# Four modulation row tiles formed by GpSimd in the first feed-forward part instead of by TensorE in the recurrent loop

## The reference, cut to what matters

```python
mod = (silu(c) @ ada_w + ada_b)        # 9 rows of 1024
(sh1, sc1, g1, sh2, sc2, g2, sh3, sc3, g3) = split(mod, 9)
y = rmsnorm(h, ffn1_pre_g) * (1 + sc1) + sh1
h = h + 0.5 * g1 * rmsnorm(swiglu(y), ffn1_post_g)
y = rmsnorm(h, mix_pre_g) * (1 + sc2) + sh2
h = h + g2 * rmsnorm(token_mix(y), mix_post_g)      # 4 mLSTM heads, 4 HGRN heads
y = rmsnorm(h, ffn2_pre_g) * (1 + sc3) + sh3
h = h + 0.5 * g3 * rmsnorm(swiglu(y), ffn2_post_g)
```

## Time and profile before

| what | us |
|---|---|
| timed runs (3): median | 1752.55 |
| timed runs: lowest, highest | 1751.01, 1753.04 |
| profiled execution: span | 1748.8 |
| PE busy in it | 1701.6 (97%) |
| DVE busy | 1133.4 (65%) |
| ACT busy | 791.6 (45%) |
| POOL busy | 349.1 (20%) |

### The profile page before, as it was taken

The page is one execution under the profiler, slowest core; times in us unless marked ns, Lnnn a source line. Parts: engine busy times, 40 slices in busy tenths (PEclk is TensorE's granted clock), DMA queues, the critical chain, the costliest instruction groups (busy, mean ns, idle before and its releaser), DMA issues.

```text
span 1748.8 us, 32936 instructions
## 1 busy us (share of the span) xinstructions
PE 1701.6 (97%) x12844; PEld 1512.7 (87%) x12844; DVE 1133.4 (65%) x1857; ACT 791.6 (45%) x1241; POOL 349.1 (20%) x325
## 2 busy tenths in 40 slices
PE   6999999999999999999899999999999999999997
PEld 3999879977999889877869999999999988888886
DVE  4877557676665455983664699488899644444444
ACT  4334454655454454642234534555544433333334
POOL 2000010111000010000010577600000155555553
PEclk9999999999999999999999999999999999999999
DMA  9877655456565533441044456545555566666664
GB/s 357 294 268 289 217 196 190 144 194 230 192 209 174 193 122 132 158 144 38 3 179 141 131 170 179 168 156 159 161 161 162 169 192 193 192 192 194 194 192 162
DMA packets 64385, 314.42 MB, mean 180 GB/s; under 512 B 7152, under 2 KB 7568, under 8 KB 44688
## 3 DMA queue, kind: packets, MB, share of 16 engines
q1 hardware_dynamic: 62928, 305.94, 52.4%
q10 hardware_dynamic: 1280, 6.82, 1.1%
q0 software_dynamic: 64, 0.04, 0.0%
HBM read 311.72 MB, written 1.05 MB: 179 GB/s over the span
## 4 chain that ended last, share of the span: by engine, by line
PE 89%; DVE 5%; ACT 2%; DMA 2%; issue 1%; POOL 1%; SPq 0%; DVEq 0%; POOLq 0%; ACTq 0%
PE bank L421 25%; PE bank L422 24%; PE bank L423 24%; PE bank L2836 2%; DMA ring<-in_stream 1%; PE bank L2809 1%; DVE ring_rounded L381 1%; PE bank L1378 1%; PE bank L2394 1%; DMA ring<-in_experts 1%; PE bank L782 1%; POOL ring_rounded L3142 1%; PE bank L2407 1%; PE bank L2045 1%; PE bank L596 0%
## 5 line engine op out<-in xcount | busy, mean ns | idle before, releaser
L423 PE MATMUL bank<-yb_rounded,ring_rounded 128*128 128x256 f32 x2000 | 566.0, 283 | 0.0
L2927 ACT CAST ring_rounded<-ring 128x1024 fp32r<-128x1024 f32 x248 | 260.5, 1051 | 281.8 <-DMA ring<-in_experts 281.6
L423 PEld LDWEIGHTS bank<-yb_rounded,ring_rounded 128*128 128x128 f32 x2000 | 383.8, 192 | 0.0
L381 DVE TENSOR_TENSOR ring_rounded<-ring,arena_rounded 128x1024 fp32r<-128x1024 f32 x230 | 270.8, 1220 | 131.3 <-ACT arena_rounded L367 130.8
L421 PE MATMUL bank<-yb_rounded,arena_rounded 128*128 128x256 f32 x1104 | 316.3, 286 | 0.9 <-issue 0.9
L422 PE MATMUL bank<-yT_rounded,arena_rounded 128*128 128x256 f32 x1104 | 313.4, 284 | 0.0
L3102 DVE TENSOR_TENSOR ring_rounded<-ring,ring_rounded 128x1024 fp32r<-128x1024 f32 x128 | 156.9, 1226 | 191.2 <-ACT ring_rounded L2927 191.2
L421 PE MATMUL bank<-yb_rounded,ring_rounded 128*128 128x256 f32 x960 | 278.1, 290 | 2.1 <-POOL ring_rounded L3142 1.2
L367 ACT CAST arena_rounded<-ring 128x1024 fp32r<-128x1024 f32 x230 | 229.0, 1048 | 106.2 <-PE bank L421 98.5
L422 PE MATMUL bank<-yT_rounded,ring_rounded 128*128 128x256 f32 x960 | 271.1, 282 | 0.0
L422 PE MATMUL bank<-ring_rounded,arena_rounded 128*128 128x512 f32 x688 | 267.7, 389 | 0.0
(11 more groups left out here) (439 smaller groups left out, 2646.4 us busy)
## 6 DMA issues: line engine op xcount, KB each, us to landing
ring<-in_stream SPq DMA_DIRECT2D x144, 1024.0 KB, 4.9
ring<-in_experts SPq DMA_DIRECT2D x256, 512.0 KB, 3.5
field<-in_stream SPq DMA_DIRECT2D x24, 512.0 KB, 7.1
field<-in_stream SPq DMA_DIRECT2D x4, 1024.0 KB, 7.0
field<-in_gains ACTq DMA_DIRECT2D x3, 512.0 KB, 7.5
field<-in_gains ACTq DMA_DIRECT2D x1, 1536.0 KB, 6.7
const<-in_const SPq DMA_DIRECT2D x1, 1473.0 KB, 11.5
xh<-in_x ACTq DMA_DIRECT2D x1, 1024.0 KB, 5.5
```

Of the source, the lines that this page charges most:

```text
L381: ins = nc.vector.tensor_tensor(ring_r[:, g % SLOTS, half], ring[:, g % SLOTS, half], top.bitcast(F32), ALU.subtract)
L423: return first, pe.matmul(bank, s_rest, m_top, start=False, stop=stop)
L2927: nc.scalar.copy(expert_top[:, n % E_SLOTS, :], expert_w[:, n % E_SLOTS, :]).then_inc(expert_top_ready, 1)
```

## The change

Tiles 12 to 15 leave the loop. A list `POOLED` takes the place of `LOOPED`. SP fetches their eight chunks, as two halves each, behind the ring chunks of the feed-forward tiles 6, 10, 14, 18, 22, 25, 27 and 29, into two places that are free at that time. GpSimd scales the four pieces of a chunk (TENSOR_SCALAR) and adds them to the row (TENSOR_TENSOR). TensorE's ones-matmuls and ACT's copies for tiles 12, 13 and 14 stand behind tiles 13, 20 and 29; those of tile 15 stand in the mixer, between the last evacuated modulation tile and the mixer's own first chunk. The ring stream is eight chunks shorter between the projections and the output projection.

```diff
-        LOOPED = {0: 12, 2: 13, 4: 14, 5: 15}
+        POOLED = [12, 13, 14, 15]
-        SUM_BEHIND = {6: 4, 10: 5, 14: 6, 18: 7, FT - 1: 8, FT + 4: 9}
+        SUM_BEHIND = {6: 4, 10: 5, 13: 12, 14: 6, 18: 7, 20: 13, FT - 1: 8, FT + 4: 9, FT + 7: 14}
+        POOL_BEHIND = [6, 10, 14, 18, 22, 25, 27, 29]
+        pool_places = [halves((arena4, 1024), (arena2, 0)), halves((arena1, 0), (arena1, HALF))]
+        def row_part_pool(pool, h):
+            tile, c = POOLED[h // 2], h % 2
+            if h == 0:
+                pool.wait_ge(sem("silu_c"), 1)
+                pool.wait_ge(sem("ada_b_in1"), 16)
+            pool.wait_ge(pool_landed[h % 2], 32 * (h // 2 + 1))
+            parts = [pool_places[h % 2][k // 2][:, k % 2 * 512:(k % 2 + 1) * 512] for k in range(4)]
+            for k, w in enumerate(parts):
+                nc.gpsimd.tensor_scalar(w, w, col("c")[:, 4 * c + k:4 * c + k + 1], 1.0, ALU.mult, ALU.mult
+                                        ).then_inc(sem("pool_row_scaled"), 1)
+            for k, w in enumerate(parts):
+                pool.wait_ge(sem("pool_row_scaled"), 4 * h + k + 1)
+                pool.wait_ge(sem("pool_row_step"), 4 * h + k)
+                nc.gpsimd.tensor_tensor(row(tile), row(tile), w, ALU.add).then_inc(sem("pool_row_step"), 1)
         def row_sum_pe(pe, tile):
-            pe.wait_ge(sem("row_step"), 8 * (HOSTED.index(tile) + 1))
+            if tile in POOLED:
+                pe.wait_ge(sem("pool_row_step"), 8 * (POOLED.index(tile) + 1))
+            else:
+                pe.wait_ge(sem("row_step"), 8 * (HOSTED.index(tile) + 1))
...
                 act.wait_ge(sem("rows_scaled"), 1)
+                act.wait_ge(sem("pool_row_step"), 4 * 7)
...
             ada_groups_pe(pe, BEHIND["ffn1"][1])
+            row_sum_pe(pe, POOLED[-1])
...
                 if i:
                     read_out(i - 1)
-                if i in LOOPED:
-                    ada_groups_pe(pe, LOOPED[i])
-                if i - 1 in LOOPED:
-                    ada_sum_pe(pe, LOOPED[i - 1], but=3)
...
             late_groups_act(act, "ffn1")
+            row_sum_act(act, POOLED[-1])
+            mark("pooled_rows", A.free, 4 + A.emptied.n)
...
-            await_mark(dve, "looped_rows")
+            await_mark(dve, "pooled_rows")
...
+                if g in pool_behind:
+                    h = pool_behind.index(g)
+                    if h >= 2:
+                        sp.wait_ge(sem("pool_row_step"), 4 * (h - 1))
+                    for place, half in zip(pool_places[h % 2], (slice(0, HALF), slice(HALF, CHUNK))):
+                        sp.dma_start(place, stream[tile_at(POOLED)[h]][:, half]).then_inc(pool_landed[h % 2], 16)
...
+            for h in range(2 * len(POOLED)):
+                row_part_pool(pool, h)
             own_rest_pool(pool, "mix")
```

More of the change, by code:

```diff
@@ L746, in partial @@
                 return arena3[:, tile * 512:(tile + 1) * 512]
-            where, at = {10: (arena3, 2048), 12: (arena2, 0), 14: (arena2, 1024), 16: (arena2, 0)}[tile - tile % 2]
+            where, at = {10: (arena3, 2048), 16: (arena2, 0)}[tile - tile % 2]
             return where[:, at + tile % 2 * 512:at + tile % 2 * 512 + 512]
@@ L957, in row_part_dve @@
                                                ALU.mult, ALU.add).then_inc(sem("row_step"), 1)
+        POOL_BEHIND = [6, 10, 14, 18, 22, 25, 27, 29]
+        pool_places = [halves((arena4, 1024), (arena2, 0)), halves((arena1, 0), (arena1, HALF))]
+        pool_landed = [sem(f"pool_row_landed{j}") for j in range(2)]
+        def row_part_pool(pool, h):
[12 more added lines that the diff above has]
+                nc.gpsimd.tensor_tensor(row(tile), row(tile), w, ALU.add).then_inc(sem("pool_row_step"), 1)
         def row_sum_pe(pe, tile):
-            pe.wait_ge(sem("row_step"), 8 * (HOSTED.index(tile) + 1))
+            if tile in POOLED:
+                pe.wait_ge(sem("pool_row_step"), 8 * (POOLED.index(tile) + 1))
+            else:
+                pe.wait_ge(sem("row_step"), 8 * (HOSTED.index(tile) + 1))
             bank = A.take(pe)
@@ L1118, in ffn_act @@
                         row_sum_act(act, SUM_BEHIND[i - 2])
-                        mark("hosted_rows", A.free, 4 + A.emptied.n)
+                        if SUM_BEHIND[i - 2] == HOSTED[-1]:
+                            mark("hosted_rows", A.free, 4 + A.emptied.n)
                 act.wait_ge(sem("rows_scaled"), 1)
+                act.wait_ge(sem("pool_row_step"), 4 * 7)
                 top_chunk_act(act, 2)
@@ L1537, in mix_act @@
                     top_chunk_act(act, 8)
-                if i in LOOPED:
-                    ada_groups_act(act, LOOPED[i])
-                if i - 1 in LOOPED:
-                    ada_sum_act(act, LOOPED[i - 1])
-                    mark("looped_rows", A.free, 4 + A.emptied.n)
             a(head_square(last - 1))
@@ L2927, in top_expert @@
                 nc.scalar.copy(expert_top[:, n % E_SLOTS, :], expert_w[:, n % E_SLOTS, :]).then_inc(expert_top_ready, 1)
-            act.wait_ge(begun, stream.shape[0] - len(own_at) - 2 * len(HOSTED))
+            act.wait_ge(begun, stream.shape[0] - len(own_at) - 2 * len(HOSTED + POOLED))
             for _ in range(2):
@@ L3181, in program @@
         source += [rest_at + i for i in (*range(1, 12), 14, 15, 12, 13)]
-        source += tile_at(LOOPED.values()) + list(range(rest_at + 16, rest_at + 20)) + tile_at(BEHIND["mix"])
+        source += list(range(rest_at + 16, rest_at + 20)) + tile_at(BEHIND["mix"])
         source += range(rest_at + 21, mix2_rows)
@@ L3185, in program @@
         source += [*range(mix2_rows + 11, mix2_rows + 29), *range(mix2_rows + 30, stream.shape[0])]
-        assert sorted(source + list(own_rows.values()) + tile_at(HOSTED)) == list(range(stream.shape[0]))
+        assert sorted(source + list(own_rows.values()) + tile_at(HOSTED) + tile_at(POOLED)) == list(range(stream.shape[0]))
         assert len(source) % SLOTS == 0
         row_behind = [split_at[0] + i + 1 for i in ROW_BEHIND]
+        pool_behind = [split_at[0] + i + 1 for i in POOL_BEHIND]
         own_behind = {split_at[FT + 4]: "mix", source.index(rest_at + 16) + 3: "ffn2", source.index(rest_at + 21) + 16: "mix2",
```

## The result

| | before | after |
|---|---|---|
| timed runs (4 each): median, us | 1751.83 | 1772.62 |
| lowest, highest | 1751.01, 1753.04 | 1769.84, 1775.28 |
| span of the profiled execution | 1748.8 | 1771.6 |
| PE busy | 1701.6 | 1703.4 |
| mean granted clock | 0.996 | 0.989 |

What follows compares the result with a forecast made beforehand. It took PE as the bound (89% of the chain), narrowly over DVE in gate/up. GpSimd rows +17, sums +3.0 and loop -7.5 gave +12.5; with 1748.8 and 3.75 carried over, 1765.0 us, range 1752 to 1774.

Steps and rivals of the forecast that it cites:

- rival A: Feed-forward part: DVE is not held up, GpSimd fits into its pauses; -4.5 us, 1748.0 us; 12 in 100.
- The loop, -7.5: Recurrent loop: 14.2 us of PE work go, 5.0 us of DVE idleness stay, so it closes 7.5 us earlier.
- rival B: The loop gives more (-12.5) and GpSimd costs less (+10), sums +3: 1753 us; 10 in 100.
- The sums, +3.0: PE's ones-matmuls: three in the feed-forward part cost 2.6 us, the fourth, in the mixer, 0.4.
- The GpSimd rows, +17: Feed-forward part: GpSimd's eight half tiles hold up DVE and thereby PE, +17 us, bounds 0 and +26.
- 14.4 was forecast: Gate/up part: the halves behind tiles 6, 10, 14 and 18 each cost PE 3.6 us.
- 2.6 was forecast for four halves: Last gate/up tile and down part: the fifth half, behind tile 22, costs 2.6 us, the last three nothing.
- The last three meet a DVE that only splits weights ... and cost nothing: Down part: beside the last three halves DVE is busy only 2.36 us in some 5.5, so cost 0.
- C: Rival: the loop gives nothing, as DVE and the ACT chain take over at once; 1772.5 us; 6 in 100.
- D: Rival: GpSimd's TENSOR_SCALAR is as dear as its TENSOR_TENSOR, rows +26; 1774 us and more; 6 in 100.
- side estimate of 7.1 us held per half tile: Feed-forward part: by the skill's 769 ns per 512 elements, a half tile holds SBUF 7.1 us, against 6.6 taken.
- The DMA queue, 0: Feed-forward part: 8.4 MB more to fetch, +46 GB/s, counted at 0, at most +2 us.

Runs made afterwards that it cites:

- e1: Changed kernel with GpSimd's 64 instructions cut to one column each, fetches, waits and sums kept: 1746.37 us, ratio 0.9978.
- e2: Changed kernel with the 64 GpSimd instructions replaced by as many MEMSETs of 128x1024, which read nothing: 1746.75 us, ratio 0.998.
- e3: Kernel before with its looped tiles and their sums left out altogether: 1742.72 us, ratio 0.9961.
- e5: Changed kernel with GpSimd's 32 additions cut to one column and the 32 scalings whole: 1746.88 us, ratio 0.9982.
- e6: Changed kernel with GpSimd's 32 scalings cut to one column and the 32 additions whole: 1762.83 us, ratio 1.0063.
- e7: Changed kernel with GpSimd's instructions of the last four half tiles one column wide, the first four full: 1757.9 us, ratio 1.0043.
- e13: Changed kernel with only tiles 12 and 13 on GpSimd, two halves in the down part and two in the mixer; 14 and 15 looped: 1748.09 us.
- e12: Changed kernel with only tiles 12 and 13 on GpSimd, three halves in the down part, the fourth in the mixer; 14 and 15 looped: 1753.35 us.
- e9: Kernel before with TensorE made to wait once, behind gate/up tile 12, for four GpSimd MEMSETs: 1752.42 us, ratio 1.0013.

## Why the prediction was right, and where it was not

**Direction and place: right.** GpSimd and VectorE alternate, L381 grows to twice its length, PE waits for it, the feed-forward part is about 28 us longer (forecast 20) and the loop shorter. The forms named in advance are there: a TENSOR_TENSOR of POOL at 1.5 us, up to 2.3, instead of 1.27, and 17.8 us of waits for L381 where some 15 were named, but 9.9 of them in the down part and only 7.9 in the gate/up part, where all were expected. e1 and e2 show the cause, and rival A is out: DVE is held up, and without it (e1, 1746.4 us) the time is near rival A's 1748.

**The loop, -7.5: right.** e3 gives 7.5 us, not the 12.5 of rival B, and leaves DVE idle 5.2 us where 5.0 were forecast. In the changed kernel's own profile it shows as -5.4, since there the clock is 0.91 over the loop: PE, which was the bound before, now waits for DVE and falls to the lower clock in between. PE's waits for DVE are the same 7.0 us in e1 and in the changed kernel; the loop takes 37.1 us at clock 1.00 (e2, e5), 38.2 at 0.96 (e1, e3) and 39.8 at 0.91 (e6, e7 and the changed kernel).

**The sums, +3.0: right within 0.7.** Measured 3.7; three of 0.85 to 0.86 us, and the fourth, counted at half, at full.

**The GpSimd rows, +17: too low, 26.2** (24.6 against its own before). This term is the step that was mis-sized, and two of its errors partly cancel.

In the gate/up part 14.4 was forecast and 11.5 measured. The delay of DVE per half was 5.0 us rather than 6.0; the scalings take less of it than I took (1.05 us in e5, forecast 4 x 0.5 x 0.91 = 1.8). PE loses only 1.7 us where it is undisturbed (halves 0 and 1 of the changed kernel), not 3.6: DVE's waits took up 1.62 + 0.75 us over two periods, and its lead all of its 1 us, not half. The halves 0 to 2 cost 5.2 us together, and the one behind tile 18 alone 6.3: a wait of 3.47 and 2.9 of the clock, in the stretches at 0.89 and 0.77. In e7's profiled execution, without a fall, the four cost 7.0: half of the forecast. So the waits were counted twice as long as they are, and the clock, which was not counted, made up for part of it.

In the down part and behind it 2.6 was forecast for four halves and 14.7 measured. The step that failed is "The last three meet a DVE that only splits weights ... and cost nothing". Only the half behind chunk 25 cost nothing. DVE also runs L923 and L924 there, beside the half behind 27, and PE waits 1.48 us behind them (1.07 in e13). At the end stand four L381 in a row, and where they are slowed (the changed kernel, e12) PE waits 3.8 us. And I had checked only that the last half ends before the end of the part, not that it pushes GpSimd's own split into those four: L381 x4 7.79 us for 4.63, then the clock at 0.66. The half beside the hosted rows made PE wait 4.66 us, with the clock at 0.92 and 0.74 around it.

**What was missing altogether** is the price of an idle TensorE beyond the wait itself. Of the +22.8 us of the spans, 12.6 are longer work for the same instructions, which the lower clock accounts for (13.4 by its own record); all of my terms were waits at the upper one. That the forecast came within 7.6 us of the time is owed in part to waits that I had counted too long. Two rivals named the time almost exactly, for reasons that are refuted: C, with 1772.5 us, had a loop without gain, and D, with 1774, TENSOR_SCALAR as dear as TENSOR_TENSOR; it takes 0.69 us for 1.27. (The side estimate of 7.1 us held per half tile is 7.0 by its own terms; nothing else uses it.)

**The DMA queue, 0: right.** e1 has all the fetches, and its gates stand at their old times but for the sums.

**The mixer, +2.2**, is 0.9 for tile 15's sum, and the rest is the clock: the fall at the mixer's start (0.66 from 280 to 290 us) stands where before has its own (0.83 from 250 to 260) but is longer. The kernel of e9, whose mixer is that of before, shows the same in its execution: 0.66 from 250 to 260 us, the mixer 124.7 us long. So neither this nor the loop's falls need the down part's halves: e7, which has those narrow, has the loop's two falls too.

What stays open: why the clock falls behind some waits and not behind others of like length. In the gate/up and down parts no wait up to 1.65 us went with a fall, and each of 2.9 us and more did; between them 1.93 (e2), 2.19, 2.34 and 2.56 us (e6) did, and 2.22 (e7) did not. That lists these runs and is no rule. In the loop, waits of 1.9 to 2.6 us went either way. That is one profiled execution of each kernel, and the runs of one kernel differ (e7's spread over 11.7 us).

## What to carry to other kernels

Work handed to GpSimd is free only where VectorE, with SBUF inputs, has more slack within one period than the delay per burst; read that slack as the wait ahead of the instruction that follows TensorE's results, and look at every instruction of VectorE in the burst, the last run of a part too. If TensorE is then left waiting, add the clock to the wait: here waits of 2.9 to 4.7 us cost another 1.7 to 2.9 each. Spread the bursts, place them where VectorE idles (the mixer, in e13), and take away only as much from the bound stage as makes the next engine the bound: two of four tiles already gave 4.5 to 5.4 us of the loop, all four 5.4 to 8.1.

## What the hardware showed that I had not expected

- MEMSETs of GpSimd, 1.0 us each and back to back for 8.3 us, do not delay VectorE's two-input instructions at all (L381 stays at 1.22 us); TENSOR_SCALAR and TENSOR_TENSOR, which read SBUF, do.
- A one-input CAST of VectorE (L415) is held up by both: 0.93 and 1.40 us for 0.29 beside the adds, and up to 1.88 beside MEMSETs (e2), though not every time. An instruction with one input in PSUM is not: 0.41.
- With one wait of TensorE of 2.9 us the clock was 0.83 over the 10 us around its end; with one of 1.2 us it stayed at 1.00.
- Costs of the same kind don't add: scalings 0.5 us, adds 16.5, both 26.2.
